# Splitting weight tiles in the head loop: tiles 4 to 7 moved from GpSimd to VectorE

## The reference, cut to what matters

```python
lower = jnp.where(strict, jnp.einsum('bhncd,bhnmd->bhncm', k_beta, k) * decay, 0.0)
a_mat = lower + jnp.eye(C, dtype=f32)
rhs = jnp.concatenate([v_beta, k_beta * jnp.exp(g)[..., None]], axis=-1)
sol = lax.linalg.triangular_solve(a_mat, rhs, left_side=True, lower=True, unit_diagonal=True)
```

## Time and profile before

| | |
|---|---|
| median of 3 runs | 1196.16 us (1194.77 to 1196.72) |
| the profiled execution's own time | 1197.76 us |
| its span in the profile | 1195.9 us |
| a head in the middle | 35.2 us |
| heads, first to last | about 90 to 364 us of the span |
| PE busy over the span | 89% |
| DVE, ACT, POOL busy over the span | 64%, 44%, 43% |

### The profile page before, as it was taken

How to read it: one execution, slowest core, us unless ns; L and a number is a source line. 1 busy time by engine, 2 the same in 40 slices (tenths; PEclk the granted TensorE clock), 3 DMA queues, 4 the chain that set the end, 5 groups by cost and what they waited for, 6 DMA issues and landing times.

```text
span 1195.9 us, 17037 instructions
## 1 busy us (share of the span) xinstructions
PE 1061.7 (89%) x5187; PEld 732.5 (61%) x5187; DVE 771.0 (64%) x1791; ACT 522.7 (44%) x1046; POOL 516.0 (43%) x407
## 2 busy tenths in 40 slices
PE   8989999999999999999979779788798797887786
PEld 6769999999998999975424325234243252342232
DVE  6527666667655666637866766676667666766656
ACT  4555666766668776412332233223322333232221
POOL 2476776666872000003533344334344343344341
PEclk9999999999999999999999999999999999999999
DMA  7443333334343455877999999999999999999997
GB/s 273 140 146 110 123 132 107 123 108 138 106 141 107 141 161 195 298 312 301 402 422 420 421 418 420 420 422 418 422 422 422 422 421 423 421 422 422 421 421 318
DMA packets 61158, 355.22 MB, mean 297 GB/s; under 512 B 7999, under 2 KB 8510, under 8 KB 27198
## 3 DMA queue, kind: packets, MB, share of 16 engines
q0 software_dynamic: 36864, 268.45, 54.2%
q1 hardware_dynamic: 24254, 86.27, 21.1%
HBM read 353.65 MB, written 1.05 MB: 297 GB/s over the span
## 4 chain that ended last, share of the span: by engine, by line
PE 51%; DMA 27%; ACT 8%; issue 7%; DVE 4%; POOL 1%; SPq 0%; DVEq 0%; POOLq 0%; ACTq 0%
DMA top<-peer_uv_dram,route 14%; DMA front<-peer_uv_dram,route 12%; PE ps L2053 12%; PE ps L1708 8%; PE ps L1710 8%; PE ps L1709 8%; PE ps L2019 4%; PE ps L2004 2%; PE ps L1866 2%; PE ps L1886 2%; ACT split L594 1%; ACT top L919 1%; DVE split L1064 1%; ACT L915 1%; ACT L908 1%
## 5 line engine op out<-in xcount | busy, mean ns | idle before, releaser
L2053 PE MATMUL ps<-top 128*128 128x512 f32 x632 | 297.7, 610 | 88.5 <-ACT top L919 88.5
L1028 POOL DMA_INDIRECT top<-peer_uv_dram,route x160 | 172.4, 1077 | 244.0 <-PE ps L2053 236.8
L2053 PEld LDWEIGHTS ps<-top 128*128 128x128 f32 x632 | 115.1, 191 | 258.0 <-ACT top L919 149.0
L1451 DVE CUSTOM_DVE_ANT_0 top<-top,scratch 128x1024 f32<-128x1024 f32 x160 | 195.9, 1225 | 119.0 <-DMA top<-peer_uv_dram,route 118.0
L1708 PE MATMUL ps<-split 128*128 128x256 f32 (+1 forms) x768 | 239.2, 311 | 4.6 <-POOL split L983 3.0
L983 POOL TENSOR_TENSOR split<-front,split 128x1024 fp32r<-128x1024 f32 x82 | 196.6, 2410 | 87.5 <-ACT split L594 86.3
L1710 PE MATMUL ps<-split 128*128 128x256 f32 (+1 forms) x768 | 224.5, 292 | 0.0
L1709 PE MATMUL ps<-split 128*128 128x256 f32 (+1 forms) x768 | 224.2, 292 | 0.0
L919 ACT ACTIVATE top<-cst,route 128x128 f32<-128x128 f32 x254 | 88.1, 394 | 256.5 <-DVE route L1459 256.5
L1028 POOL DMA_INDIRECT front<-peer_uv_dram,route x64 | 66.0, 1030 | 267.9 <-DVE route L1582 170.2
L594 ACT ACTIVATE split<-front 128x1024 fp32r<-128x1024 f32 x128 | 133.4, 1055 | 102.5 <-PE ps L1710 80.7
(11 more groups left out here) (321 smaller groups left out, 1579.3 us busy)
## 6 DMA issues: line engine op xcount, KB each, us to landing
front<-in_tiles_dram SPq DMA_DIRECT2D x80, 512.0 KB, 3.3
front<-branch_tiles_dram SPq DMA_DIRECT2D x24, 512.0 KB, 4.2
front<-in_w_in_dram SPq DMA_DIRECT2D x8, 512.0 KB, 4.7
front<-in_w_mem_kv_dram SPq DMA_DIRECT2D x8, 512.0 KB, 3.6
front<-kv_tiles_dram SPq DMA_DIRECT2D x8, 512.0 KB, 3.4
top<-in_w_out_dram SPq DMA_DIRECT2D x8, 512.0 KB, 6.8
rest<-peer_w_q_by_head_dram SPq DMA_DIRECT2D x3, 1024.0 KB, 8.9
gate_part<-peer_w_q_by_head_dram SPq DMA_DIRECT2D x3, 1024.0 KB, 14.7
```

Of the source, the lines that this page charges most:

```text
L1028: pool.indirect_dma_start(rows_uv[k % RING], None, peer_uv, bass.IndirectOffsetOnAxis(ap=idx[c][:, k:k + 1], axis=0)).then_inc(s_row[k % R ...
L1451: dve.tensor_tensor_reduce(out=row, in0=row, in1=h2[:, c, :], scale=1.0, scalar=0.0, op0=ALU.mult, op1=ALU.add, accum_out=acts[c][:, k:k + ...
L2053: ins = pe.matmul(ps[:, 2 * c + half, :], diag[:, k % 8, :], rows_uv[k % RING][:, D + half * 512:D + (half + 1) * 512], start=False, stop= ...
```

## The change

POOL makes the low parts of tiles 0 to 3 alone. DVE makes those of tiles 4, 5 and 6 in levels 4, 5 and 6, between the taps of the convolution and the wait for Z, and that of tile 7 behind `w1`, ahead of `att_parts` (in the last head there is no tile 7). POOL gets one wait, for the low part of the head's last tile, ahead of the next head's tile 0.

```diff
@@ POOL, head @@
-                for i in range(3, 7 if last else 8):
-                    low(*tile(i))
+                low(*tile(3))
                 if not last:
                     mask_decays(h + 1)
+                pool.wait_ge(lo_ready, made(*tile(6 if last else 7)))
                 low(*of_head(h + 1, 0))
@@ DVE, head, in the loop over levels s @@
                         convolved(h + 1)
+                    if s > 3:
+                        low(*of_head(h, s))
                     on(dve, "lvlZ", h * (LEVELS - 1) + (s - 1))
@@ DVE, head, behind the levels @@
                 dve.tensor_tensor(w1, dv[:, P:T], ps[:, 3, 0:P], ALU.subtract).then_inc(done("w1_ready"), 1)
                 if not last:
+                    low(*of_head(h, 7))
                     att_parts(h + 1)
```

## The result

| | before | changed |
|---|---|---|
| median of 5 runs | 1196.72 us (1194.77 to 1199.16) | 1214.23 us (1211.20 to 1215.78) |
| profiled execution | 1197.76 us | 1211.20 us |
| its span | 1195.9 us | 1209.4 us |
| a middle head | 35.18 us | 37.57 us |

The ratio of the changed kernel to the one before is 1.0145, with a 95% interval of 1.0129 to 1.0161: 17.5 us slower by the medians. The forecast was 1211.6 us in a range of 1206.5 to 1215.5.

The account below looks back on a forecast made before the run. PE's instruction stream was taken to set the time of the heads; 0.87 + 1.14 + 0.18 = 2.19 us in seven heads plus 0.1 makes 15.4 us, added to the median 1196.16: 1211.6 us, range 1206.5 to 1215.5.

Parts of the forecast that it names:

- three signs of being wrong: PE's load of Y not moving against its filling, line 1064 above 1.23 us in the heads, or DVE waiting for line 594.
- Level 4: Tile 4's low part on DVE delays the subtraction of Z, so PE's load of the next Y waits 0.87 us.
- Level 5: Tile 5's low part delays the subtraction of Z with no slack, so PE waits the full 1.14 us.
- Level 6: Tile 6's low part delays DVE's chain by 0.18 us, which PE waits ahead of `cross`; no wait at `sol0`.
- Tile 7: Its low part ahead of `att_parts` costs nothing, as low part and `att_parts` take 1.83 us where `att_parts` took 1.94.
- The rival in which it keeps its 1.94 us: `att_parts` on DVE stays at 1.94 us; PE's load for its sum is 0.73 us later per head, 1216.7 us; chance 0.05.
- Last head: No taps there; low parts delay subtractions in levels 5 and 6, PE's slack takes most: 0.1 us, estimated.
- upper bound: With 1.23 us per low part and 0.1 us for each semaphore wait, 2.7 us per head, 1215 us.
- No change: Low parts would sit wholly in DVE's wait for Z and cost nothing: 1196.2 us; chance 0.03.
- faster: A relieved POOL would shorten PE's stretches at Z by 0.5 us per head: 1192.7 us; chance 0.03.
- One level only: Level 4's slack on PE is above 1 us, so one level costs 1.14 us per head: 1204.2 us; chance 0.05.
- Late tiles: A transfer lands late, a high part is missing and the inverse waits, 1 us per head: 1218.6 us; chance 0.04.

Follow-up runs that it names:

- before_fill3: The kernel before with three steps of filling between Y and Z in every level instead of two, nothing of the change; ratio 1.0222, a middle head of 38.62 us.
- before_two: The kernel before with one step of filling more between Y and Z in levels 5 and 6; ratio 1.0148, a middle head of 37.38 us.

## Why the prediction was right

*The mechanism.* As forecast, PE waits twice per head for the subtraction of Z, and once shortly for the copy of the first solution. A middle head was forecast at 37.4 us and is 37.57.

None of the three signs of being wrong is there: line 1064 takes 1.23 us at most in the heads, DVE has no wait for line 594 in them, and the load of Y did move against the filling before it.

*Level 4*: forecast 0.87 us, measured 0.80 alone. *Level 5*: forecast 1.14, measured 1.31 alone. This is the term that was mis-sized most. I let the low part start where the subtraction had started, behind 0.15 us of waiting for the taps; it started after 0.30, and the run with the low parts ahead of the taps got the 0.15 back. *Level 6*: forecast 0.18, measured 0.29 alone. The low part started 0.04 us behind the copy's end, not 0.08 before it, which makes the difference. *Tile 7*: forecast nothing, measured 0.02, with line 1264 at 0.68 us. The rival in which it keeps its 1.94 us is refuted: the 1.94 us was a wait for a GpSimd operation, and went with it. That is as the Trainium skill's page "SBUF — State Buffer", section "SBUF: two separate sides", has it. *Last head*: forecast 0.1 us. Between the two profiles the last masking of the decays is 13.40 us later than before, and DVE's first sums for the memory attention, behind the last head, 13.46 us: 0.06 us for the last head.

*The sum.* 2.39 us in seven heads is 16.7 us, where I had 15.3. The two medians are 17.5 us apart; the interval of the ratio reaches from 15.4 to 19.3 us and holds both. The measured time lies 2.6 us above the forecast, in the upper part of the range. What covered the terms that were too small was the upper bound, which had 0.1 us for every semaphore wait of a low part. At the low end the range had 1.7 us to spare under the forecast's bounds, not the 1 us that I wrote.

*The profiled executions* are only 13.4 us apart (their spans 13.5), and the trace says where the rest is. The changed one reached the first masking of the decays 1.8 us earlier (78.55 against 80.36 us), ahead of anything that the change touches: in the 14 profiles of this study this point lies at 78.5 to 79.0 us in eight and at 80.1 to 80.4 in six, whatever the version; why is open. And its first head won a race that the other lost, worth 1.5 us (below): from the first to the second masking it took 0.89 us more than before, not 2.39. 16.7 - 1.8 - 1.5 + 0.1 = 13.5.

*The rivals.* No change and faster fell with the ratio. "One level only" fell with tiles 4 and 5 alone, which both cost. Late tiles fell with tile 4 alone. What the Trainium skill's page "GPSIMD Engine Reference", section "Engine selection", states on the choice of engine is true of the operation (2.395 against 1.225 us) and was no guide to the time: PE did not wait for the slower engine, but it did for the faster one.

## What to carry to other kernels

Before moving work to the engine that does it faster, find that engine's idle time at the very place, between what it waits for and who waits for it: here 1.22 us of work cost between 0.02 and 1.31 us by its place, on an engine that was 64% busy. When moving filling, ask what the place it is taken from covers, and what will start earlier because of it: in these runs an earlier start of work that nobody waits for cost up to 2 us per head.

## What the hardware showed that I had not expected

**POOL and DVE exclude each other in more forms than the one I had counted.** The cast of line 1257, with a single input, took 0.42 us alone and 1.83 beside POOL's subtraction; line 1259, with two inputs, 0.69 and 2.75. The few elements of line 1197 took 0.16 us in the middle heads and 2.05 in those of `before_fill3`. POOL is held up as well when DVE comes first: in `before_two` its subtraction beside the cast took 2.66 us instead of 2.39. The copy of Y and the subtraction of Z, which have an input in PSUM, kept their 0.42 us beside POOL.

**Such a meeting can be a race that falls either way.** In the first head line 1202 of DVE and a subtraction on POOL become ready within 0.02 us of each other. The timeline of DVE in the kernel before:

```profile
93.34 2.69 DVE L1202 TENSOR_TENSOR rest<-cst,scratch 128x256 f32<-128x256 f32 x1
```

and in the changed one:

```profile
91.52 0.41 DVE L1202 TENSOR_TENSOR rest<-cst,scratch 128x256 f32<-128x256 f32 x1
```

POOL's subtraction starts at 93.34 and 91.54. PE waited 1.46 us for line 1202 in the one and not in the other. Four of the 14 profiles of this study have a 2.69 us instance, changed or not; so part of the scatter of a few microseconds among runs of one kernel may be this, which was not tested.

**A place in a queue can cost 0.15 us by itself.** Behind DVE's wait for its own taps in level 5, the subtraction of Z alone started 0.15 us after the taps, and the low part 0.30 us after them. Ahead of the taps the same low part started without a gap, and the head was 0.14 us shorter. What in the queue takes that time is open.
